# Expert units of a hybrid encoder: the first gate and up step of every row class as a short piece behind the comparisons, with an announced jump to the rest

## The reference

```
def moe_swiglu(h, w_router, w1, w3, w2):
    logits = jnp.einsum('nd,de->ne', x, w_router)
    top_logit, top_e = lax.top_k(logits, TOP_K)          # 2 of 8 experts
    gates = jax.nn.softmax(top_logit, axis=-1)
    ...                                                  # tokens sorted by expert
    yb = lax.map(expert_block, (xb, block_e))            # (silu(x w1) * (x w3)) w2
    y = jnp.zeros_like(x).at[sorted_tok].add(sorted_gate[:, None] * yb[dest])
```

## Time and profile before

| | |
|---|---|
| median of 3 runs | 2550.61 us (2550.46 to 2551.18) |
| profiled execution | 2548.87 us, span 2547.2 us |
| TensorE busy | 2463.3 us, 97% of the span |
| VectorE, ScalarE, GpSimd busy | 660.9, 508.0, 116.2 us |
| mean DMA traffic | 189 GB/s |

### The profile page before, as it was taken

The page is one execution under the profiler, slowest core; times in us unless marked ns, Lnnn a source line. Parts: engine busy times, 40 slices in busy tenths (PEclk is TensorE's granted clock), DMA queues, the critical chain, the costliest instruction groups (busy, mean ns, idle before and its releaser), DMA issues.

```text
span 2547.2 us, 38676 instructions
## 1 busy us (share of the span) xinstructions
PE 2463.3 (97%) x16200; PEld 2154.0 (85%) x16201; DVE 660.9 (26%) x1405; ACT 508.0 (20%) x1034; POOL 116.2 (5%) x100
## 2 busy tenths in 40 slices
PE   8999998999999999899989999999989999999998
PEld 5668746888886578648989999999989999999996
DVE  2256543334742366522000000010000010100104
ACT  2145512222421255411001001011010010100102
POOL 2021100000001030101000000000000000000001
PEclk9999999999999999999999999999999999999999
DMA  8200444333220210436885656767767777788873
GB/s 261 83 34 15 131 149 129 99 99 124 74 103 27 83 48 1 152 124 227 298 308 195 225 199 233 296 258 297 290 249 263 286 281 289 286 312 298 317 295 134
DMA packets 202896, 482.29 MB, mean 189 GB/s; under 512 B 4833, under 2 KB 31600, under 8 KB 202336
## 3 DMA queue, kind: packets, MB, share of 16 engines
q1 hardware_dynamic: 192240, 430.41, 46.1%
q0 software_dynamic: 8304, 40.82, 5.1%
q10 hardware_dynamic: 2176, 8.39, 0.8%
HBM read 460.98 MB, written 35.39 MB: 195 GB/s over the span
## 4 chain that ended last, share of the span: by engine, by line
PE 80%; issue 2%; DVE 2%; ACT 0%; DMA 0%; POOL 0%; DVEq 0%; POOLq 0%; ACTq 0%
PE ps L922 34%; PE ps L937 17%; PE ps L821 10%; PE ps L657 6%; PE ps L832 5%; PE ps L665 3%; PE ps L773 2%; PE ps L650 2%; PE ps L890 1%; PE ps L906 1%; DVE x_rows L1628 0%; DMA rows_by_slot<-attention_arena,gains 0%; PE ps L753 0%; PE ps L754 0%; ACT attention_arena L1035 0%
## 5 line engine op out<-in xcount | busy, mean ns | idle before, releaser
L922 PE MATMUL ps<-hT,attention_arena 128*128 128x132 f32 (+3 forms) x4096 | 524.2, 286 | 22.8 <-issue 21.9
L922 PEld LDWEIGHTS ps<-hT,attention_arena 128*128 128x128 f32 x4096 | 509.1, 192 | 24.7 <-issue 24.7
L1618 DVE TENSOR_TENSOR attention_arena<-ps,attention_arena 128x256 f32<-128x256 f32 x224 | 95.1, 425 | 1205.2 <-ACT attention_arena L1211 1205.2
L922 PE MATMUL ps<-hT,weight_ring 128*128 128x132 f32 (+3 forms) x3072 | 389.6, 283 | 0.0
L922 PEld LDWEIGHTS ps<-hT,weight_ring 128*128 128x128 f32 x3072 | 377.6, 190 | 0.0
L1211 ACT ACTIVATE attention_arena<-ps 128x256 f32<-128x256 f32 x224 | 86.0, 384 | 1130.8 <-PE ps L922 1130.7
L937 PE MATMUL ps<-attention_arena 128*128 128x132 f32 (+3 forms) x2048 | 266.8, 284 | 0.8 <-DVE attention_arena L1618 0.8
L657 PE MATMUL ps<-weight_ring,hT 128*128 128x384 f32 (+3 forms) x768 | 256.5, 494 | 3.3 <-DVE hT L1240 1.7
L937 PEld LDWEIGHTS ps<-attention_arena 128*128 128x128 f32 x2048 | 254.6, 190 | 1.0 <-DVE attention_arena L1618 1.0
L657 PEld LDWEIGHTS ps<-weight_ring,hT 128*128 128x128 f32 x768 | 145.7, 192 | 105.6 <-issue 60.2
L821 PE MATMUL ps<-x_high,w_parts 128*128 128x512 f32 x704 | 223.1, 398 | 5.7 <-ACT x_high L1106 5.7
(11 more groups left out here) (203 smaller groups left out, 1831.9 us busy)
## 6 DMA issues: line engine op xcount, KB each, us to landing
attention_arena<-in_e_w_dram SPq DMA_DIRECT2D x96, 2048.0 KB, 12.3
weight_ring<-in_e_w_dram SPq DMA_DIRECT2D x72, 2048.0 KB, 12.2
weight_ring<-in_w_dram SPq DMA_DIRECT2D x22, 1024.0 KB, 7.0
weight_ring<-in_w_dram SPq DMA_DIRECT2D x4, 2816.0 KB, 10.0
weight_ring<-in_w_o_dram SPq DMA_DIRECT2D x4, 2048.0 KB, 8.8
attention_arena<-rows_by_slot POOLq DMA_DIRECT2D x8, 1024.0 KB, 11.4
results_by_slot<-attention_arena ACTq DMA_DIRECT2D x8, 1024.0 KB, 9.4
weight_ring<-in_w_in_dram SPq DMA_DIRECT2D x2, 3072.0 KB, 10.6
```

Source lines behind the costliest of these rows:

```text
L922: last = nc.tensor.matmul(ps[:, f % 2, m * UNIT:m * UNIT + n], w[:, k, i * P:(i + 1) * P], XT[:, k, 0:n], start=(k == 0), stop=(k == ND - 1))
L1618: tt(eh[:, f % EHS, :], ps[:, f % 2, UNIT:2 * UNIT], esil[:, f % 2, :], ALU.mult).then_inc(gu_free, 1)
```

## The change

Each class's body is cut in two. The starts, `start_of_unit_of_up_to_n`, hold only the wait for the unit's rows and the gate and up step 0; the fifteen starts follow each other directly behind the comparisons. Each start opens with a hint for its own last branch, which jumps to `rest_of_unit_of_up_to_n`, the other 27 gate and up steps, all down steps and the transposes. The fifteen rests follow behind all starts, and end as the bodies did.

```diff
-            def unit_body(u, n):
+            def unit_start(u, n):
 
                 pe.wait_ge(turn_out, u * 8 + (4 + GIVEN_TURN))
-                for f in range(FE):
+                gate_up_step(u, 0, n)
+
+            def unit_rest(u, n):
+
+                for f in range(1, FE):
                     if f == FE - 1:
                         pe.addr_align(256, offset=80, max_nops=0)
                         back = pe.mark_branch_hint_location()
...
-                    if f:
-                        down_step(u, f - 1, n)
+                    down_step(u, f - 1, n)
...
             for i, n in enumerate(CLASSES[:-1]):
                 with nc.body(f"over_{i}", valid_engines=only_pe):
-                    pe.br_lt(held, n + 1, on_true=body_of(n), on_false=f"over_{i + 1}")
+                    pe.br_lt(held, n + 1, on_true=start_of(n), on_false=f"over_{i + 1}")
             with nc.body(f"over_{len(CLASSES) - 1}", valid_engines=only_pe):
-                pe.br(body_of(CLASSES[-1]))
+                pe.br(start_of(CLASSES[-1]))
             for n in CLASSES:
-                with nc.body(body_of(n), valid_engines=only_pe):
+                with nc.body(start_of(n), valid_engines=only_pe):
                     u = pe.snap(at_unit, min_val=0, max_val=NU - 1)
-                    back = unit_body(u, n)
+                    ahead = pe.mark_branch_hint_location()
+                    unit_start(u, n)
+                    pe.br(rest_of(n)).branch_hint(ahead)
+            for n in CLASSES:
+                with nc.body(rest_of(n), valid_engines=only_pe):
+                    u = pe.snap(at_unit, min_val=0, max_val=NU - 1)
+                    back = unit_rest(u, n)
                     pe.addr_align(256, offset=255, max_nops=0)
                     pe.br("unit_next").branch_hint(back)
```

More of the change, by code:

```diff
@@ L962, in _, with start_of, rest_of @@
             only_pe = [mybir.EngineType.PE]
-            def body_of(n):
-                return f"unit_of_up_to_{n}"
+            def start_of(n):
+                return f"start_of_unit_of_up_to_{n}"
+            def rest_of(n):
+                return f"rest_of_unit_of_up_to_{n}"
             pe.reg_mov(at_unit, 0)
```

## The result

The changed kernel takes 2592.74 us (median of 4 runs, 2587.04 to 2594.93) against 2550.8 us before: 1.0161 of it, 95% interval 1.0143 to 1.0179. The direction was forecast; the size was not: +42 us where +16 was said, outside the range of 2551 to 2583. The profiled execution has a span of 2591.7 us, 44.5 more than before.

What follows compares the result with a forecast made beforehand. TensorE's own time and its stops were taken to bound the kernel. Class 132 (+16.8), the first unit (+2.5) and the other classes (-1.4) gave +17.9 us on 2548.87, with 1.7 for the median 2568.5, shaded to 2567; range 2551 to 2583.

Steps and rivals of the forecast that it cites:

- One block is read ahead; a target outside costs a fetch.: Jumps into unit bodies: only the next instruction block is read ahead; other targets cost some 5.8 to 7.05 us.
- Class 132, the new stop.: Between start and rest of 132-row units: the rest's fetch leaves a new stop of 2.1 to 3.4 us, taken as 3.0.
- The extra on top.: Behind the new stop in 132-row units: a late following block or low clock, 0 to 2.5 us, taken as 1.2.
- First unit: First 132-row unit: 4.2 us less waits of 0.9 and 0.8 us that cover or absorb part of it, so 2.5.
- Classes 144 and 148, first jump.: Jump into these starts: first matmul some 4.1 us beyond on time instead of 5.8 and 6.85; 1.7 and 2.7 won.
- Their second jump.: Start to rest in classes 144, 148, 176: fetch hidden, or stops of 2.6, 1.6 and 1.2 us; 1.0 each taken.
- Rival 2: At each of eight jumps: the late hint is no help, the jump asks again, 2.5 us each; 2587 us, chance 0.11.
- Rival 3: Blocks 1 to 4 are all there once block 0 is entered, so three classes' stops go: 2528 us, chance 0.06.
- Rival 1: At the starts' hints: a hint is much quicker than a missed jump, stops 0 to 1 us; 2546 to 2551, chance 0.13.

Runs made afterwards that it cites:

- two and three steps: Changed kernel with two gate and up steps per start, hint kept, end code moved: 2571.11 us; with a third and the first down step added: 2556.83 us.
- hint moved up: Changed kernel with the hint of class 132 put ahead of the read of the unit's row count, given in every unit: 2577.75 us.

## Why the prediction was wrong, step by step

- *One block is read ahead; a target outside costs a fetch.* Right. The packets looked at in these runs fit it, and class 176 kept its first stop (7.84 us; 7.49 before).
- *Class 132, the new stop.* This step failed. The prediction let the price of a miss, 5.8 to 7.05 us beyond on time, run from the hint, since it stood where the missed jump had stood, and so counted the start's 3.7 us of matmuls as cover: 3.0 us left. The runs show that a hint at this place is served only some 7.5 us behind the unit's first matmul (two and three steps), so that in the changed kernel the jump came first, 2.1 us behind the hint, and paid in full: it lasts 6.2 to 6.9 us in the later four units. And of the start's 3.7 us of matmuls only the last 2.2 cover it. From the unit's first matmul to the rest's first it took 8.15 to 8.8 us in the later four, not 6.7: stops of 4.3 to 4.9. Over four units that is 6.4 us of the miss (18.4 against 12.0). A small slip beside it: the 5.8 us of class 144 takes 0.20 us as on time where the two others take 0.44; by their measure it is 5.6.
- *The extra on top.* Taken as 1.2 a unit between bounds of 0 and 2.5, it was the low clock in each of the four, 9.9 us together against 4.8. 3.1 and 2.7 us, in two of them, lay above the bound. First unit: 2.5 said, 1.3 measured.
- *Classes 144 and 148, first jump.* Nearly right: the first matmul came 4.3 us behind the last unit's end at 144 and 5.3 at 148, where 4.1 beyond on time was said (on time being 0.20 to 0.44 behind that end).
- *Their second jump.* Wrong, and the second largest error: 1.0 us each was taken between a hint served first (0) and one served behind the read-ahead (1.2 to 2.6). The packets, at 1553.0 to 1553.5 and 1557.0 to 1557.5 for the unit of 144 rows, look like the latter, but the second comes no later without hints (6.6 to 7.3 us behind the first matmul of the three units, 6.9 to 7.3 with them). So here too the jump asked for the rest, and the hint did nothing. The stops were 3.3 to 4.05, and the clock fell a second time, on which no term was spent: -1.4 said for the three, +11.0 measured.
- *Rivals.* Rival 2 had the time nearly right (2587) and half of the mechanism: the late hint is no help and the jump asks. But it does not ask again, in line behind the hint's fetch; there is one packet for each target. Rival 3 falls with the packets. Rival 1 has it backwards: a hint close behind the entry to a block is slower than a missed jump, not quicker (7.6 to 8.3 us from the hint to its packet with two and three steps in the later four units, 3.5 to 4.2 from the jump to its own without hints).

In sum: 19.3 said for class 132 against 29.6, -1.4 for the others against +11.0.

Two points stay open: why a hint right behind the comparisons needs 7.6 to 8.3 us to its packet, the one ahead of the read of the row count, given 1.4 us sooner, 4.8 to 5.4 us, and the one at step 27 of the kernel before 1.2 to 1.4 us in three of its units; and by what share of the changed kernel's spread (2587 to 2595) the clock's falls vary from run to run.

## What to carry to other kernels

A hint right behind the entry to a block needs about 11 us here (some 8 to the packet and 2.7 to work). One at step 27, 9 to 11 us ahead of its jump, hid the whole fetch; how much less would do there was not tried. A piece of work put in front of a jump that has no hint in time covers only the 2.2 us that TensorE still has to run, however long the piece is (32 and 64 matmuls of 132 rows). Look for the place where the target is first known, not for the last one at which it can still be told. A stretch of code that runs straight on needs no announcement, so a cut through the commonest path must be paid for before it gains. Count the jumps on every path, and for each the lead in microseconds from the hint to the jump.

## What the runs showed of the hardware that was not expected

A jump without a hint costs the same stop behind 32 matmuls as behind 64 (4.0 to 4.7 and 4.2 to 4.4 us), as the sequencer is 2.2 us ahead of the end of TensorE's work both times. The stops of 4 us were followed by low clock as those of 7 had been: behind each of the eight in the later units of 132 rows, with and without hints, the group of 32 matmuls took 5.4 to 6.9 us instead of 3.76. In the unit of 144 rows two stops of 4.32 and 3.97 us lost 3.3 us by the clock, the one of 6.03 us before 2.0. Of the stops near 2 us (hint moved up) three of four left the clock at 1.00, of those of 2.6 to 3.1 us (two steps with the hint) two of four. The Trainium skill says in Runtime: NRT & Kernel Launch ("Instruction fetch mechanics") that a taken branch outside a two-block window stalls for a fetch; these runs agree, and put the stall at 4.7 to 6.7 us of the sequencer for the jumps without hints, against 0.33 to 0.44 us where the block was there (three steps).
